# Long convolution: the order of the vector work in the spectrum product, and of the side branch and the merge around it

## What is computed

```python
u = short_conv(hy_in, w_short[l], b_short[l])
v_h, x1, x2 = jnp.split(u, 3, axis=-1)
k_spec = hyena_filter_spectra(...)
zc = v_h
for o, gate in enumerate((x1, x2)):
    zc = gate * long_conv(zc, k_spec[:, o], hy_bias[l, o])
u_hy = (zc * jax.nn.silu(z_hy)) @ w_hy_out[l]
...
u_attn = (attn * jax.nn.silu(z_attn)) @ w_attn_out[l]
gates = jax.nn.sigmoid(jnp.concatenate([gate_hy, gate_attn], axis=-1) + b_gate[l])
merged = g_hy * u_hy + g_at * u_attn
x = x + merged @ w_out[l]
```

## Time and profile before

| | us |
|---|---|
| median of 3 runs (lowest, highest) | 1777.75 (1777.62, 1779.82) |
| the profiled execution | 1780.19 |
| its span in the profile | 1778.4 |
| PE busy | 1748.8 (98%), 7776 matmuls |
| DVE busy | 1044.0 (59%) |
| POOL busy | 719.2 (40%) |
| ACT busy | 637.8 (36%) |

### The profile page before, as it was taken

How to read it: one execution, slowest core, us unless ns; L and a number is a source line. 1 busy time by engine, 2 the same in 40 slices (tenths; PEclk the granted TensorE clock), 3 DMA queues, 4 the chain that set the end, 5 groups by cost and what they waited for, 6 DMA issues and landing times.

```text
span 1778.4 us, 21432 instructions
## 1 busy us (share of the span) xinstructions
PE 1748.8 (98%) x7776; PEld 1407.0 (79%) x7776; DVE 1044.0 (59%) x1181; ACT 637.8 (36%) x891; POOL 719.2 (40%) x303
## 2 busy tenths in 40 slices
PE   7999999999999999999999999999999999999999
PEld 6887788887788888888787788887876667787887
DVE  6777466765653365376775466784425653858541
ACT  5222222225544755322222222223445644333321
POOL 2443344434422421444344344444453443444443
PEclk9999999999999999999999999999999999999999
DMA  5332222334211220332333233322521014222243
GB/s 177 105 101 98 83 95 96 109 97 168 83 60 60 87 68 25 101 124 95 122 104 99 80 114 96 105 94 87 183 81 30 32 36 178 83 95 95 95 133 116
DMA packets 45231, 172.88 MB, mean 97 GB/s; under 512 B 5177, under 2 KB 5177, under 8 KB 44380
## 3 DMA queue, kind: packets, MB, share of 16 engines
q1 hardware_dynamic: 39888, 150.75, 26.1%
q10 hardware_dynamic: 5260, 20.94, 3.3%
HBM read 161.05 MB, written 10.62 MB: 97 GB/s over the span
## 4 chain that ended last, share of the span: by engine, by line
issue 62%; PE 18%; POOL 16%; DVE 1%; ACT 1%; POOLq 1%; DMA 0%; SPq 0%; DVEq 0%; ACTq 0%
POOL wlo L258 16%; PE psum L292 5%; PE psum L294 5%; PE psum L293 5%; PE psum L1577 1%; POOLq L266 0%; PE psum L1566 0%; PE psum L1538 0%; DMA xT<-x_dram 0%; ACT whi L280 0%; PE psum L1532 0%; DVE small L1848 0%; POOLq L256 0%; ACT mprob L1727 0%; DVE merged_hi L1272 0%
## 5 line engine op out<-in xcount | busy, mean ns | idle before, releaser
L258 POOL TENSOR_TENSOR wlo<-raw,whi 128x1024 fp32r<-128x1024 f32 (+3 forms) x266 | 677.0, 2546 | 983.1 <-ACT whi L280 983.0
L280 ACT ACTIVATE whi<-raw 128x1024 fp32r<-128x1024 f32 (+3 forms) x267 | 291.9, 1094 | 729.8 <-PE psum L294 723.7
L292 PE MATMUL psum<-h_hi,whi 128*128 128x512 f32 x1360 | 539.0, 396 | 7.0 <-POOL wlo L258 3.8
L294 PE MATMUL psum<-h_hi,wlo 128*128 128x512 f32 x1360 | 530.6, 390 | 0.0
L293 PE MATMUL psum<-h_lo,whi 128*128 128x512 f32 x1360 | 530.3, 390 | 0.0
L292 PEld LDWEIGHTS psum<-h_hi,whi 128*128 128x128 f32 x1360 | 256.0, 188 | 67.1 <-issue 8.7
L293 PEld LDWEIGHTS psum<-h_lo,whi 128*128 128x128 f32 x1360 | 255.9, 188 | 55.0 <-issue 3.1
L294 PEld LDWEIGHTS psum<-h_hi,wlo 128*128 128x128 f32 x1360 | 255.8, 188 | 54.1
L292 PE MATMUL psum<-mid_hi,whi 128*128 128x512 f32 x352 | 138.1, 392 | 0.0
L293 PE MATMUL psum<-mid_lo,whi 128*128 128x512 f32 x352 | 137.0, 389 | 0.0
L294 PE MATMUL psum<-mid_hi,wlo 128*128 128x512 f32 x352 | 137.0, 389 | 0.0
(11 more groups left out here) (339 smaller groups left out, 2448.7 us busy)
## 6 DMA issues: line engine op xcount, KB each, us to landing
raw<-wk_dram SPq DMA_DIRECT2D x220, 512.0 KB, 3.7
raw<-wd_dram SPq DMA_DIRECT2D x32, 704.0 KB, 4.1
raw<-wp_dram SPq DMA_DIRECT2D x8, 640.0 KB, 3.9
spectra_scratch<-spec_out ACTq DMA_DIRECT2D x8, 512.0 KB, 7.3
x_scratch<-xT ACTq DMA_DIRECT2D x2, 2048.0 KB, 7.5
xT<-x_scratch ACTq DMA_DIRECT2D x8, 512.0 KB, 4.7
spec<-spectra_scratch ACTq DMA_DIRECT2D x2, 2048.0 KB, 10.2
raw<-wq_dram SPq DMA_DIRECT2D x8, 320.0 KB, 2.9
```

What stands on the lines that cost most here:

```text
L258: pool.tensor_tensor(wlo[s][:, 0:w], raw[s][:, 0:w], whi[s][:, 0:w].bitcast(F32), ALU.subtract).then_inc(lo_ready, 1)
L280: act.activation(whi[s][:, 0:w], raw[s][:, 0:w], ACT.Copy).then_inc(hi_ready, 1)
L292: pe.matmul(dst, s_hi, m_hi, start=start and i == 0, stop=False, **kw)
L294: last = pe.matmul(dst, s_lo, m_hi, start=False, stop=stop and i == n - 1, **kw)
```

## The change

On DVE, in each step of each long convolution: each pair of products is followed at once by the sum of the two, behind a wait for the products, where before all eight products came first and the four sums after them. The two counters of products (`prod`, `upper_prod`) become one that counts 8 in a step. The partial sums of the merge (`vector_part`) of step 1 stand in front of the halves' sums, and no longer behind them. The side branch of step 0 is taken apart: `sides` stands between the lower half (products and sums) and the upper half, `vector_z` (now z's product alone) behind the upper half, and the product into x2z is a method of its own, which runs in step 1 between the two halves. The x2z product of step 1, till now in front of the second `vector_part`, comes behind it.

```diff
@@ class HyenaInputs
             def vector_z(self, dve, i, b):
                 dve.wait_ge(self.sig, i + 1)
                 dve.tensor_tensor(zsilu, zsilu, b, ALU.mult).then_inc(self.silu, 1)
+
+            def vector_x2z(self, dve, i):
                 dve.wait_ge(self.silu, i + 1)
                 dve.wait_ge(self.conv, 9 + i)
                 dve.tensor_tensor(x2z[:, i, :], x2z[:, i, :], zsilu, ALU.mult).then_inc(self.x2z, 1)
@@ class LongConvolution
                 act.wait_ge(unit_done, self.unit_forth(j) + 1)
                 if n:
-                    act.wait_ge(self.upper_prod, 4 * n)
+                    act.wait_ge(self.prod, 8 * n)
@@
-            def multiply(self, eng, signal, k, x, dst):
-
-                for d, (a, b) in zip(dst, ((0, 0), (1, 1), (0, 1), (1, 0))):
-                    eng.tensor_tensor(d[:, :], k[a], x[b][:, :], ALU.mult).then_inc(signal, 1)
-
-            def vector_upper(self, dve, j):
-                self.multiply(dve, self.upper_prod, self.spectrum(j)[2:], self.even_sum, self.upper)
+            def vector_product(self, dve, n, k, x, dst):
+                upper = dst is self.upper
+                first = 8 * n + 4 * upper
+                pairs = ((0, 0), (1, 1), ALU.subtract), ((0, 1), (1, 0), ALU.add)
+                for i, (one, other, op) in enumerate(pairs):
+                    for d, (a, b) in zip(dst[2 * i:2 * i + 2], (one, other)):
+                        dve.tensor_tensor(d[:, :], k[a], x[b][:, :], ALU.mult).then_inc(self.prod, 1)
+                    dve.wait_ge(self.prod, first + 2 * i + 2)
+                    dve.tensor_tensor(dst[2 * i][:, :], dst[2 * i][:, :], dst[2 * i + 1][:, :], op).then_inc(self.y, 1)
@@
                     if n:
-                        dve.wait_ge(self.prod, 4 * n)
+                        dve.wait_ge(self.prod, 8 * n)
                         dve.wait_ge(self.ready, 4 * n)
+                    if j:
+                        merge2.vector_part(dve, 2 * o, 4 * o + 2)
                     for i in range(2):
@@
-                    if j:
-                        merge2.vector_part(dve, 2 * o, 4 * o + 2)
-                    self.multiply(dve, self.prod, self.spectrum(j)[:2], low, lower)
+                    self.vector_product(dve, n, self.spectrum(j)[:2], low, lower)
                     dve.wait_ge(self.halves, 4 * n + 4)
                     if n:
                         dve.wait_ge(self.f32, 4 * n)
-                    self.vector_upper(dve, j)
                     if j == 0:
                         hyena_in.sides(dve, 8 + n, self.side_bank(0))
+                        self.vector_product(dve, n, self.spectrum(j)[2:], high, upper)
                         hyena_in.vector_z(dve, n, self.side_bank(1))
-                    for i, (half, signal) in enumerate(((lower, self.prod), (upper, self.upper_prod))):
-                        dve.wait_ge(signal, 4 * n + 4)
-                        dve.tensor_tensor(half[0][:, :], half[0][:, :], half[1][:, :], ALU.subtract).then_inc(self.y, 1)
-                        dve.tensor_tensor(half[2][:, :], half[2][:, :], half[3][:, :], ALU.add).then_inc(self.y, 1)
+                    else:
+                        hyena_in.vector_x2z(dve, n - 1)
+                        self.vector_product(dve, n, self.spectrum(j)[2:], high, upper)
                     dve.wait_ge(self.y, 4 * n + 4)
@@
                 merge2.vector_part(dve, 2 * o + 1, self.forth(1))
+                hyena_in.vector_x2z(dve, 2 * o + 1)
                 for j in range(5):
```

More of the change, by code:

```diff
@@ L2266, in build @@
         class LongConvolution:
-            signals = [sem(f"long_{x}") for x in ("even", "halves", "products", "upper_products", "spectrum", "f32",
+            signals = [sem(f"long_{x}") for x in ("even", "halves", "products", "spectrum", "f32",
                                                   "hi", "ready", "back", "gated", "gated_hi", "out")]
@@ L2281, in __init__ @@
                 self.o = o
-                (self.even, self.halves, self.prod, self.upper_prod, self.y, self.f32, self.hi, self.ready, self.back,
+                (self.even, self.halves, self.prod, self.y, self.f32, self.hi, self.ready, self.back,
                  self.out32, self.out_hi, self.out) = LongConvolution.signals
```

## The result

The change makes the kernel slower. In five runs each, the changed kernel has a median of 1787.63 us (1784.98 to 1787.76), the kernel before 1779.82 (1777.62 to 1780.39); the ratio is 1.0043 with a 95% interval of 1.0029 to 1.0057. The profiled execution took 1787.76 us, its span is 1786.0: 7.6 more than before. I had forecast 4.4 more. The medians lie 7.8 apart, and the changed one 9.9 above the 1777.75 that I had started from.

The account below looks back on a forecast made before the run. PE was taken to bound the kernel. A new wait for z's product (+7.5), partial sums earlier (-2.1) and a smaller POOL wait (-1.0) gave +4.4, so 1777.75 became 1782.1 us, range 1777.0 to 1784.2.

Parts of the forecast that it names:

- What bounds the kernel: PE, busy 1748.8 of 1778.4 us; DVE's order counts only where PE waits for DVE or something DVE delays.
- the new wait: Group 3 of `tensor_forth(1)`, both convolutions: PE waits for z's product, ending near 1534.8; 3.75 each, +7.5 us.
- POOL's second hold: Upper half, step 0: POOL holds the first sum to 1532.25; with the first stop alone 1.7 us lost, not 3.75.
- The price of an idle stretch: PE's waits: beyond idle time, 0.25 us added for each wait removed and 0.1 for each one made.
- The starting point: Whole kernel: profiled execution 1780.19 us lies 2.4 above the median, so the sum was added to 1777.75.
- Part 2: Step 1: partial sums in front of the halves' sums remove PE's wait for them; -2.1 us.
- Part 3: Step 1, sum after pair, x2z between: PE's wait for POOL's `wlo` shrinks; -1.0 us, bounds 0 and -2.3.
- rival A: POOL gets in at the running instruction's end, so its wait goes entirely, -2.3; +3.1 in all, 1780.9 us; chance 0.27.
- Part 4: x2z of step 1 behind the second partial sums, before the output products: costs nothing; uncovered, at most 0.3 us.
- what gives nothing back: Behind PE's wait for z's product nothing recovers the loss; the `Y_lo` wait of 0.71 us remains, moving with PE.
- D: Output remainders or a late sum of step 1 also reach PE, 0.5 to 1 us each; 1783.8 us; chance 0.08.
- C: POOL holds only one of the halves: loss 1.7 twice, in all -1.0 to +0.3, 1777.5 us; chance 0.10.

Follow-up runs that it names:

- E1: Changed kernel with z's product of step 0 put back in front of the upper half; median 1773.7 us, ratio 0.9976 to the kernel before.
- E3: Kernel before with only z's product of step 0 (x2z behind it) moved behind the four sums; median 1789.1 us, ratio 1.0058 to before.
- E7: Changed kernel with POOL making 64 of 1024 columns of one weight remainder in each long convolution; median 1777.8 us, ratio 0.9991 to before.
- E2: Kernel before with only the merge's partial sums moved in front of the halves' sums of step 1; median 1774.4 us, ratio 0.9978 to before.
- E4: Changed kernel with z's product of step 0 behind the first sum of the upper half; median 1777.2 us, ratio 0.9992 to the kernel before.
- E6: Kernel before with only the pairing, each sum behind its two products, sides and z's product behind both halves; median 1788.8 us, ratio 1.0056 to before.
- E11: Kernel before with one dependent wait added on DVE behind the first of step 1's four sums; median 1777.4 us, ratio 0.9991 to before.
- E8: Kernel before with partial sums first, ACT's `Y_hi` of step 0 one weight unit earlier, x2z moved into step 1; median 1773.5 us, ratio 0.9964 to before.
- E10: Kernel before with partial sums first and ACT's `Y_hi` of step 0 one weight unit earlier; median 1774.0 us, ratio 0.9969 to before.

## Why the prediction was wrong

**What bounds the kernel, and the new wait: right.** z's product ends where I had put it, PE idles 3.5 us twice as forecast, and E1, E3 and E7 confirm the place, the mechanism and the share of POOL's second hold. The loss of 3.75 each is 3.76 by the same count (3.51 + 0.25).

**The price of an idle stretch: the step that failed.** I took 0.1 for going on after a wait ("I add ... 0.1 to each one made"). That is the price at full clock. The stretch shows +7.4 against -4.6 of gains (E2) and +7.5 of waits; 4.5 remain. It is the clock: behind its two new waits PE takes 2.80 and 1.59 longer for the same work than in E4, where the wait is 1.57 and the clock stays full, together 4.4. The trace of before had it in two places that I had not looked at: behind the idle stretches of 2.07 at 854 and 2.15 at 1338:

```profile
856.00:858.00 2.00, 2.00 (x6) 1.55 (x5) 1.74 (x3) 0.00 (x0) 2.00 (x1) 0.50 0.00 0
```

Two lines of the page hide it: a clock given in tenths of 40 slices, and a mean of 0.997. With +4.4 for the clock my sum would have been +8.8 and the median 1786.5. That this comes near the measured 1787.63 would have been luck: +8.8 is 1.4 above the stretch's +7.4, and the starting point was too low.

**The starting point: a second miss.** I added to 1777.75, the median of three runs of which two lay in the lower group, though the execution that I had profiled, 1780.19, lay in the upper one. I took the 2.4 between them for something to subtract. Four of the changed kernel's five runs lie at 1786.8 to 1787.8 with clocks of 0.994 and 0.995, one at 1784.98 with 0.996, and the profiled one has the half clock near 1338 as that of before has. Like against like it is 1787.76 against 1780.19, so some 2.4 of the miss of 5.5 in the median are this. But 1780.19 + 4.4 = 1784.6 is 3.2 short too: the missing price of the clock decides.

**Part 2, the partial sums: right**, -2.1; E2 shows the wait gone, without a new one.

**Part 3: sized wrong, the rival A was right here.** I took -1.0; the whole wait went, -2.3 by its idle time and -2.5 by what E2 leaves for it. In the changed kernel POOL asks at 1558.03, 0.04 in front of a dependent sum, and gets in at once:

```profile
1558.03 2.40 POOL L258 TENSOR_TENSOR wlo<-raw,whi 128x1024 fp32r<-128x1024 f32 x1 [4.04 <-ACT whi L280]
```

I had put the request 0.1 behind the start of that sum; it came 0.04 in front of it, and these 0.14 us decided. Nor was pairing needed for the gain: in E2, without it, the wait goes as well, since POOL asks sooner. It is enough for it, as E6 shows, where the partial sums stay in their old place. The mechanism (a run of DVE work keeps POOL out until a dependent gap) is shown by E11 for the run of sums; for the run of products it does not hold (E2, and 1523.68 in the earlier trace rows). What sets the two apart stayed open. The Trainium skill (SBUF — State Buffer, section Who interferes with whom) has the first to issue keep the ports for its whole instruction. E2's POOL instruction, 0.35 longer, agrees with that; the 5.12 of before, 2.7 longer over several DVE instructions of 0.68, does not.

**Part 4 and what gives nothing back: right.** No wait for `yb_lo` or the output, and the wait for `Y_lo` stays at 0.7, moved with PE; that it hangs on ACT's order was shown by E8 and E10.

**The rivals.** None of them had the clock in it; D reached only to 1783.8. All my cases for the loss ended in the idle time itself, and so did the upper end of the range. Its lower end is not the middle of C, as I wrote: C's terms give -1.0 to +0.3, whose middle is 1777.4 and not 1777.0.

## What to carry to other kernels

Where PE is always busy, look up in the trace what an instruction that PE waits for has as slack (here 1.24 us) before anything is put in front of it, and count with it what POOL holds back. A new idle stretch of PE can cost more than its own length: look behind the idle stretches that the trace already has for half clock, since it made +7.5 into +12. The gain of a change that does several things can lie in one of them: here it came with two instructions moved, and the rest was worth nothing or less. And where the executions of a kernel fall into two groups, take the starting point and the trace from the same one.

## What the runs showed of the hardware

- PE idle for 1.43, 1.47 (at 45 us) and 1.57 us: full clock behind it. Idle for 2.07, 2.18, 2.99, 3.5 and 4.37: the clock at 0.50 behind it in every trace here, for 3.4 or 6.8 us, which costs 1.5 to 1.7 or 2.8. Between 1.57 and 2.07 nothing was measured. One execution of E4 without a trace, 1774.18 us at a mean clock of 1.000, suggests that the half clock behind 2.07 can be missing too. Idle for 2.15 at 1338: half clock in some traces, none in others of kernels that are the same up to there.
- A longer idle stretch did not cost more clock: 1.6 behind 4.37, 2.8 and 1.6 behind 3.5. In the changed kernel the clock fell once 0.8 us before PE went on and once 0.8 us behind it.
- A wait on DVE that costs 0.12 let POOL in 1.8 us earlier (E11). Which runs of DVE instructions keep POOL out is open: a run of four sums did, runs of products did not.
